# A hand-written interleaving string: 666 of 1452 places get another number of attention half-steps

## What is computed

```python
s = einsum('bqhrd,bkhrd->bhrqk', qb, kb) * scale           # two score maps r per head
p = softmax(where(mask, s, -inf))
attn = p[:, :, 0] - lam * p[:, :, 1]                       # differential attention
...
log_1mb = where(mask, log_sigmoid(-z), 0.0)                # stick-breaking
suffix = cumsum(log_1mb, reverse=True) - log_1mb
a = where(mask, exp(log_sigmoid(z) + suffix), 0.0)
```

## Time and profile before

| what | value |
|---|---|
| median of 3 executions | 3809.48 us (3808.88 to 3811.32) |
| the profiled execution | 3808.88 us, of which 3807.1 us are the span from first to last instruction |
| mean granted TensorE clock | 0.989 of full |
| matmuls, weight loads | 21288 each |
| DVE, ACT, POOL instructions | 4115, 3455, 704 |

### The profile page before, as it was taken

How to read it: one execution, slowest core, us unless ns; L and a number is a source line. 1 busy time by engine, 2 the same in 40 slices (tenths; PEclk the granted TensorE clock), 3 DMA queues, 4 the chain that set the end, 5 groups by cost and what they waited for, 6 DMA issues and landing times.

```text
span 3807.1 us, 55010 instructions
## 1 busy us (share of the span) xinstructions
PE 3645.8 (96%) x21288; PEld 3193.3 (84%) x21288; DVE 1885.8 (50%) x4115; ACT 1696.7 (45%) x3455; POOL 797.5 (21%) x704
## 2 busy tenths in 40 slices
PE   7999889999999999999999999999999999999998
PEld 6888878888878988888889987888879978888897
DVE  4346564545657654456655545334567752111433
ACT  4334544555655554455543435334455542111322
POOL 3444333454444431100010101110000000000100
PEclk9999999999999999999999999999999999999999
DMA  6887667676776667445454455555454464555444
GB/s 164 267 251 213 192 178 254 224 273 247 261 255 214 238 212 291 173 172 183 171 188 148 167 198 192 183 177 185 149 205 137 151 222 179 192 182 207 167 175 147
DMA packets 327701, 760.01 MB, mean 200 GB/s; under 512 B 52625, under 2 KB 212369, under 8 KB 271122
## 3 DMA queue, kind: packets, MB, share of 16 engines
q1 hardware_dynamic: 266386, 720.83, 54.4%
q10 hardware_dynamic: 61056, 35.67, 3.5%
HBM read 581.00 MB, written 175.39 MB: 199 GB/s over the span
## 4 chain that ended last, share of the span: by engine, by line
PE 56%; DVE 5%; ACT 2%; issue 1%; DMA 1%; POOL 0%; SPq 0%; ACTq 0%; DVEq 0%
PE PS L1375 15%; PE PS L1377 15%; PE PS L1376 15%; PE PS L1483 2%; PE PS L1493 2%; PE PS L1474 1%; PE PS L1475 1%; PE PS L1507 1%; PE PS L1453 1%; DMA GB<-scratch_YS 1%; DVE GB L1935 0%; DVE PP L2093 0%; DVE SM L2018 0%; DVE BIG L1947 0%; ACT BIG L1670 0%
## 5 line engine op out<-in xcount | busy, mean ns | idle before, releaser
L1375 PE MATMUL PS<-WF,BIG 128*128 128x256 f32 (+1 forms) x2328 | 722.7, 310 | 15.8 <-POOL WF L2322 6.5
L1376 PE MATMUL PS<-WF,BIG 128*128 128x256 f32 (+1 forms) x2328 | 709.8, 305 | 0.0
L1377 PE MATMUL PS<-WF,BIG 128*128 128x256 f32 (+1 forms) x2328 | 709.8, 305 | 0.0
L1375 PE MATMUL PS<-BIG,WF 128*128 128x512 f32 (+1 forms) x1792 | 686.4, 383 | 11.2 <-DVE BIG L1947 6.4
L1377 PE MATMUL PS<-BIG,WF 128*128 128x512 f32 (+1 forms) x1792 | 675.5, 377 | 0.0
L1376 PE MATMUL PS<-BIG,WF 128*128 128x512 f32 (+1 forms) x1792 | 675.1, 377 | 0.0
L2322 POOL TENSOR_TENSOR WF<-RAW,WF 128x512 fp32r<-128x512 f32 x380 | 507.3, 1358 | 707.9 <-ACT WF L1613 707.9
L1375 PEld LDWEIGHTS PS<-WF,BIG 128*128 128x128 f32 x2328 | 448.1, 192 | 39.7 <-ACT BIG L1659 6.5
L1376 PEld LDWEIGHTS PS<-WF,BIG 128*128 128x128 f32 x2328 | 448.6, 193 | 20.5 <-issue 1.4
L1377 PEld LDWEIGHTS PS<-WF,BIG 128*128 128x128 f32 x2328 | 448.1, 192 | 18.3
L1375 PEld LDWEIGHTS PS<-BIG,WF 128*128 128x128 f32 x1792 | 342.2, 191 | 72.0 <-issue 8.7
(11 more groups left out here) (225 smaller groups left out, 6369.7 us busy)
## 6 DMA issues: line engine op xcount, KB each, us to landing
WF<-scratch_WS SPq DMA_DIRECT2D x264, 1024.0 KB, 5.0
scratch_WS<-WF SPq DMA_DIRECT2D x110, 1024.0 KB, 6.6
W<-scratch_WS SPq DMA_DIRECT2D x66, 1024.0 KB, 4.9
RAW<-in_w_in SPq DMA_DIRECT2D x84, 512.0 KB, 4.2
KV<-scratch_KS SPq DMA_DIRECT2D x60, 512.0 KB, 5.7
QQ<-scratch_QS SPq DMA_DIRECT2D x192, 128.0 KB, 5.0
XH<-in_x SPq DMA_DIRECT2D x32, 512.0 KB, 6.1
scratch_QS<-STG ACTq DMA_DIRECT2D x96, 128.0 KB, 4.0
```

What stands on the lines that cost most here:

```text
L1375: pe.matmul(o, Ah, Bh, start=first, stop=False)
L1376: pe.matmul(o, Ah, Bl, start=False, stop=False)
L1377: return pe.matmul(o, Al, Bh, start=False, stop=last)
```

## The change

The string `HALF_STEPS` gets other digits. Both strings have 1452 digits with the sum 749 and 977 zeros, so the same half-steps are taken, in the same order among themselves, and the projections keep theirs; only the place at which a half-step stands among the projections changes. 666 places have another digit. The number of half-steps taken up to a place differs between the strings by at most 13, mostly by less than 4. Nothing else in the program is touched, and no other step is added or removed.

```diff
--- before.py
+++ after.py
@@ -207,21 +207,21 @@
 
 
 HALF_STEPS = (
-    "0000000000000000000000000000000000000000000000000000000000000000000000000001001000012021111112011000"
-    "2000202121101221000121209241300100000003031403130520400001202021010020200200000010300000011100102100"
-    "0000100200001001200021011000300020010010000100111001000100022010010100001011001110003110000000001011"
-    "4002100020200000010311310312010112100002100000000011001041000010010001110211020311101000002010010000"
-    "1100100100021130105020020210000101110010000000000010000000010000010011000030000100200110000100000410"
-    "0202000000010000110001000100101000301000010000020000000010010100000110011000030020000020000002000000"
-    "0060000201000000100200010000000000010122000100020000002005500020012005040002010200000030000001010011"
-    "0101002000100010302022010000020000001100001010101110000001201113033010101201001011001002000010000001"
-    "0101000210301011021122200001001000000000000102002000001102304003200100200200000000110000000000100000"
-    "0000000102010000110010000000000000000300000000000001010011204200203110000211000001000000000030301000"
-    "1000000010020001000000000010000003000000100000001010100510001301041101000000100001100000010000110130"
-    "3000001112200021020000010100020000000011000000001000001012110000200022001001110001003230200220120200"
-    "0001102210012110000020000000100100020010210001011210010100002010101010000000010010000020000200102201"
-    "0031110000010010000000001000000000021100001001000110101011001020003110000000201110200000003000010021"
-    "0100300011111200000200120001030000001000032202001317"
+    "0000000000000000000000000000000000000000000000000000000000000000000000000010000000021102002112000202"
+    "0110222020004000220002027a32000201300000030102020137130020112001000201000013000000000002000010111111"
+    "3010000103000100000000220100100002102100021000000000000001001211000001100112010021302100110108000200"
+    "0011010011001000000200212110102003000100020100100011030001100011000201011110211110220001101010100000"
+    "0100100010020121421210101021100010100100000000000001000000000000001020020000110000000012011000001012"
+    "0000010013110000100000010002005100000000000000100100000020000000020011001000000022010010000000000001"
+    "0010000100100000001000002000000020101041301112010014010010002000031025800200000001011030000010100020"
+    "0000001001101000010111220300010000000200000200021010020010001101314111210200100100100001000000010101"
+    "0110010011211020211003001100100011001000001000001021100321060002000100011011000100000010000100010001"
+    "0000000200000100020000001000000000000310010000100000020101001100002121114100000000010110000000000001"
+    "1000010010020003000001020002010000000000000000010020006030000301010000020000000120000010000001001010"
+    "0100002021000101310000001103120100002000010230000211200101001000000002000040102000000002220000000024"
+    "1201031210001002010010110000000100000100100021000210102012101100001001010010001101003001000200001110"
+    "2100130010002000000001000000000001001000110000000100100020200100301200010011010102220010010010000000"
+    "3001010001113000100201101000021010001000000100922025"
 )
 
 
```

## The result

The kernel with the new string takes 3869.32 us (median of 4 runs, 3866.61 to 3873.05), the one before, measured beside it, 3810.4 us (4 runs): a ratio of 1.0154, with an interval of 1.0137 to 1.0172. It is slower by 59 us, where I had predicted 8 us faster.

The account below looks back on a forecast made before the run. TensorE, with a matmul in flight for 3645.8 of 3807.1 us, was taken as the bound, so only its idle time and clock could move. The terms summed to -8.3 us; 3800.5 us was predicted, with 3786 to 3820 holding 8 in 10.

Parts of the forecast that it names:

- g: All other places, where half-steps move by a few places: -3 us, bounds -10 and +8.
- f: Burst of 9 half-steps at place 1446, last heads: PE waits on DVE's chains, +4.5 us, bounds 0 and +8.
- d: End of the first softmax pass, digits at 120 to 124: part of PE's 4.3 us of waits goes, -2.3 us.
- a: First scores, places 74 to 83: PE's wait for the queries' DMA goes, -2.9 us, bound 0 to -2.9.
- b: Around place 163: two exps taken ahead of `put_v`'s DMA issues, both PE waits go, net -4.7 us.
- c: Clock from 606 to 624 us, 0.81 before: all of its loss regained, -3.4 us, bounds 0 and -3.4.
- stage borders that no digit touches: PE's waits where activations are turned between stages: a third of its idle time, taken as fixed.
- All three signs: Clock well off 0.989; PE waits for L2096, L2050, L1724 up over 10 us in sum; L1453 borders moved over 5.
- e: Stick-breaking burst at places 124 to 126, digits 7 10 3: 9 us of waiting for 5.5, +3.5 us, bounds 0 and +8.
- Rival 2: DVE in the bursts, at every large digit: slower, 3818 to 3821 us, chance 0.2.
- Rival 1: Whole kernel: waits only change their places, no change, about 3808 us, chance 0.22.
- Rival 3: Bursts at 125 and 1446 lower TensorE's clock: 6.8 us added, about 3807 us, chance 0.13.

Follow-up runs that it names:

- e4: Kernel before with its old digits of places 180 to 1433 taken two places later: 3953.39 us, +142 us (1.0371).
- e11: Kernel before with its old digits of places 180 to 1434 taken one place later: +98.9 us (1.0267).
- e16: Kernel before with its old digits of places 182 to 1435 taken one place earlier: +75.8 us (1.0201).
- e6: Kernel before with the new digits at places 74 to 83, and place 162's two half-steps put ahead of its DMA issues: -0.8 us (0.9999).
- e12: Kernel before with the new digits at places 120 to 143 alone (7 10 3 at 124 to 126 among them): +6.8 us (1.0024).

## Why the prediction was wrong

The step that failed is **g, "the rest"**: -3 us with bounds of -10 and +8. Of the 61 us in the traces about 5 belong to f and about 8 to the burst at 124 to 126 with what d gave back, a took 2 to 4 off, and b with c changed nothing. That leaves some 50 us for g. I had traced the larger waits of *before* and priced their removal. I had not looked at the places where before did not wait, and that is where the new string pays: places 480 to 509 had 1.3 us of excess and have 13.3, 270 to 299 had 0.7 and have 6.1. One such place in after, PE, DVE and POOL:

```profile
1304.71 0.66 PE L1483 MATMUL PS<-CB,PP 128*128 128x128 f32 x4 [2.17 <-DVE PP L2044]
```

```profile
1300.24 2.07 DVE L2202 TENSOR_SCALAR XS<-XS,SM 128x128 f32<-128x128 f32 x4
1302.35 1.65 DVE L2206 TENSOR_TENSOR XS<-XS,GROW 128x512 f32<-128x512 f32 x1
1303.92 0.74 DVE L2044 SCALAR_TENSOR_TENSOR PP<-PP,SM 128x512 f32<-128x512 f32 x1
```

```profile
1300.93 2.52 POOL L2322 TENSOR_TENSOR WF<-RAW,WF 128x512 fp32r<-128x512 f32 x2 [6.46 <-ACT WF L1613]
```

The new string takes three half-steps at 509, where the old one takes none between 504 and 510. The last row names something that I had overlooked. L2202 and L2206 take 2.07 and 1.65 us here; in e4 they take 1.11 and 0.69. That is 1.9 us of this wait of 2.17, and a POOL instruction (L2322) runs beside them. In the whole trace of after 153 DVE instructions take over 0.15 us longer than the lower quartile of their line and shape, 107 us more in sum, and every one of them overlaps a POOL instruction, as 737 of the 4115 do; before, it is 123 instructions and 83 us, again without exception. So DVE's 24.9 us of added busy time come with DVE and POOL overlapping at other instructions than before. How much of the loss is due to that, no run here separates.

The bounds of g were drawn from the digits' statistics (fewer clusters of 3 to 5, more of 6 and up), as if any place were as good as another. e4, e11 and e16 show what an arbitrary change of neighbours is worth: 76 to 142 us. The upper bound of g should have been of that size.

The same step had a second gap: it priced half-steps alone and took the projections' own waits as fixed ("stage borders that no digit touches"). They grew by 21 us, the half-steps' by 18. All three signs that the prediction named for being wrong appeared: a clock of 0.983 for 0.989, waits for DVE L2096, L2050 and ACT L1724 that grew by 14.5 us in sum (over 10), and waits of L1453 for L1947 that grew by 6.3 us (over 5).

Point by point:

- *a, first scores, -2.9.* Right: the wait for QQ is gone, after is 4.0 us ahead by place 80, and in e6 the stretch gains 2.2.
- *b, place 163, -4.7, and c, its clock, -3.4.* Wrong, both 0 (e6). Their bound of 0 was right, but not by its reason, another block of issues behind the exps. The named waits went, but ACT was still issuing DMAs, and the weights' split took the exps' place in the queue.
- *d, -2.3.* Wrong. The waits of the earlier trace rows are gone, but a turn at 439.92 us waits 4.08 us for L1967.
- *e, the burst at 125, +3.5.* Too small, and near in its waits by luck: 9 us predicted, and the five rows shown for 465 to 480 us sum to 8.3, but 4.12 of that is the projections' eviction wait, which the term doesn't name. The burst's own six waits sum to 5.3 us. The clock was missing too: with both, e12 measured +6.8 us for d and e.
- *f, the burst at 1446, +4.5.* Right in mechanism and size. PE waits 1.04 + 1.40 + 1.40 + 2.10 = 5.9 us for a chain on DVE that comes round in 3.3 us (6 and 3.35 predicted), and the delay grows by 5 us. PE, then one round of DVE:

```profile
3117.68 0.71 PE L1507 MATMUL PS<-PT,KV 128*128 128x256 f32 x4 [1.04 <-DVE PT L2050]
...
3120.23 0.50 PE L1474 MATMUL PS<-KV,QQ 128*128 128x512 f32 x1 [1.40 <-DVE PP L2096]
...
3123.47 0.50 PE L1474 MATMUL PS<-KV,QQ 128*128 128x512 f32 x1 [1.40 <-DVE PP L2096]
...
3127.52 0.72 PE L1507 MATMUL PS<-PT,KV 128*128 128x256 f32 x4 [2.10 <-DVE PT L2050]
```

```profile
3117.45 0.68 DVE L2079 SCALAR_TENSOR_TENSOR PP<-PS,PP 128x512 f32<-128x512 f32 x1
3118.16 1.28 DVE L2093 TENSOR_TENSOR_SCAN PP<-SM,PP 128x512 f32<-128x512 f32 x1
3119.48 0.69 DVE L2096 TENSOR_TENSOR PP<-PS,PP 128x512 f32<-128x512 f32 x1
3120.09 0.68 DVE L2050 TENSOR_TENSOR PT<-PS,PT 128x512 fp32r<-128x512 f32 x1
```

- *The rivals.* Rival 2 came nearest: its five more places with 6 or more half-steps were priced at 22 us, and the stretches of 30 places that hold 125, 293, 670, 859 and 1446 gained 7.4 + 5.4 + 2.0 + 2.9 + 5.3 = 23 us of excess. Its total was too low for the same reason as mine, since the other 38 us sit elsewhere, 5 of them in the stretches with the large digits at 151 and 1054 and the rest at digits of 1 to 5. Rival 1 held for b and c. Rival 3 held at 125 (8.5 us of clock lost there, where it had 3.4 more than before in mind) and over the whole program: 22 us of clock. The Trainium skill ("TensorE: Matmul & The Clock Gate", section "HAM oscillation — how this bites in real kernels") says that idle gaps are paid for again in matmuls at half rate. These rows agree with it: 39 us more of waits came with 22 us more lost by the clock.

What is settled: where the loss lies, that its parts add up, that neither cluster size, nor lateness, nor the first burst explains it, and that DVE's falling behind is enough to make waits of this kind. DVE ends 34 of the 39 us of added waits; that is the profile's account by the last release, and DVE can itself be late through ACT or POOL. What stays open: what makes DVE late at each place. The cut of the normalizations was too small to tell, nothing was run without POOL's work beside DVE, and no ACT pad over 3.7 us was tried.

## What to carry to other kernels

When a change moves many small things in a tuned order, price what it may break before what it mends: the sites that don't wait now are the larger sum, and a shift of everything by one place shows in one run how large. A wait that is taken away in front of a busy queue (here ACT issuing DMAs for 8 us) reappears at the next instruction that needs this queue; follow the queue, not the waiting instruction. And read slack as a length: here DVE could mostly be 3.6 us behind unnoticed, and twice that cost its full length at two of three places.

## What the runs showed that I had not expected

- Waits repeat to a hundredth of a microsecond. In e12 the six waits of the burst are 0.71, 0.76, 0.98, 0.72, 0.34 and 1.75 us, the same six as in after, 3.7 us earlier.
- Nearly the same order of work, one place earlier or later, costs 2.0 or 2.7% (e16, e11).
- 14 DMA issues on ACT's queue held it for 8.39 us in e6 and, at the same work in after, for 9.62 us.
